# A fourth buffer for the weights of the second mixer's attention, and other copiers

## The reference, cut to what matters

```
q_r = rope_partial(q, cos, sin); k_s = rope_partial(k_s, cos, sin); k_w = rope_partial(k_w, cos, sin)
...
p = masked_softmax(jnp.einsum('bqghd,bkgd->bghqk', qb, kb) * scale, mask)
return jnp.einsum('bghqk,bkgd->bqghd', p.astype(vb.dtype), vb)
...
o = gate[..., 0:1] * heads(o_cmp) + gate[..., 1:2] * heads(o_sel) + gate[..., 2:3] * heads(o_win)
return (o.reshape(B, S, NSA_INNER) * jax.nn.silu(z)) @ w_out
```

## Time and profile before

| | |
|---|---|
| median of 3 runs | 1896.23 us |
| time of the profiled execution | 1899.72 us |
| its span | 1898.0 us |
| PE busy in the span | 1824.1 us (96%) |
| DVE, ACT, POOL busy | 1095.2, 675.3, 308.9 us |
| attention of this mixer | 626.14 to 775.6 us of the span |
| PE busy from 626 to 776 us | 125.51 us |

### The profile page before, as it was taken

The page is one execution under the profiler, slowest core; times in us unless marked ns, Lnnn a source line. Parts: engine busy times, 40 slices in busy tenths (PEclk is TensorE's granted clock), DMA queues, the critical chain, the costliest instruction groups (busy, mean ns, idle before and its releaser), DMA issues. The chain is left out here.

```text
span 1898.0 us, 36850 instructions
## 1 busy us (share of the span) xinstructions
PE 1824.1 (96%) x15870; PEld 1484.7 (78%) x15870; DVE 1095.2 (58%) x1644; ACT 675.3 (36%) x1100; POOL 308.9 (16%) x292
## 2 busy tenths in 40 slices
PE   8999999999999788999999899999999999999997
PEld 6877757688888567778888669888878888888886
DVE  4664354553257788444366887778574635354545
ACT  4334332332223577442222374433233322122342
POOL 4210011130002565320021240000001000000011
PEclk9999999999999899999999999999999999999998
DMA  5334323142223010134421100002042322322221
GB/s 191 103 111 134 136 83 133 45 190 101 90 74 111 35 37 12 49 109 138 137 102 56 48 2 4 4 3 70 4 178 92 104 104 89 111 89 89 78 100 45
DMA packets 42848, 160.87 MB, mean 85 GB/s; under 512 B 5312, under 2 KB 14528, under 8 KB 28096
## 3 DMA queue, kind: packets, MB, share of 16 engines
q1 hardware_dynamic: 28480, 143.84, 22.1%
q10 hardware_dynamic: 14208, 14.68, 2.2%
HBM read 140.42 MB, written 16.78 MB: 83 GB/s over the span
## 5 line engine op out<-in xcount | busy, mean ns | idle before, releaser
L257 DVE TENSOR_TENSOR wlo<-raw,whi 128x2048 fp32r<-128x2048 f32 (+2 forms) x113 | 251.0, 2221 | 179.2 <-ACT whi L248 178.8
L248 ACT ACTIVATE whi<-raw 128x2048 fp32r<-128x2048 f32 (+2 forms) x113 | 209.0, 1850 | 320.8 <-PE ps L283 161.4
L281 PE MATMUL ps<-act_hi,whi 128*128 128x512 f32 x616 | 243.1, 395 | 0.0
L301 PE MATMUL ps<-act_lo,whi 128*128 128x512 f32 x632 | 242.7, 393 | 0.0
L283 PE MATMUL ps<-act_hi,wlo 128*128 128x512 f32 x616 | 240.6, 391 | 0.0
L282 PE MATMUL ps<-act_lo,whi 128*128 128x512 f32 x616 | 240.5, 390 | 0.0
L300 PE MATMUL ps<-act_hi,whi 128*128 128x512 f32 x592 | 236.4, 399 | 0.0
L305 PE MATMUL ps<-act_hi,wlo 128*128 128x512 f32 x632 | 156.5, 389 | 0.0
L301 PEld LDWEIGHTS ps<-act_lo,whi 128*128 128x128 f32 x632 | 120.2, 190 | 25.9 <-issue 1.2
L305 PEld LDWEIGHTS ps<-act_hi,wlo 128*128 128x128 f32 x632 | 118.6, 188 | 24.7
L300 PEld LDWEIGHTS ps<-act_hi,whi 128*128 128x128 f32 x592 | 111.6, 188 | 32.5 <-issue 8.2
(11 more groups left out here) (550 smaller groups left out, 3474.7 us busy)
## 6 DMA issues: line engine op xcount, KB each, us to landing
raw<-stream_in SPq DMA_DIRECT2D x107, 1024.0 KB, 4.9
v_scratch<-v_out ACTq DMA_DIRECT2D x16, 256.0 KB, 3.5
z_scratch<-zt ACTq DMA_DIRECT2D x16, 256.0 KB, 2.9
mlh_v<-v_scratch SPq DMA_DIRECT2D x4, 1024.0 KB, 4.8
mlh_z<-z_scratch SPq DMA_DIRECT2D x16, 256.0 KB, 2.6
cmp_w<-cmp_w_in SPq DMA_DIRECT2D x2, 2048.0 KB, 11.3
z_scratch<-in_zt ACTq DMA_DIRECT2D x16, 256.0 KB, 3.2
mix_g<-z_scratch SPq DMA_DIRECT2D x16, 256.0 KB, 6.6
```

What stands on the lines that cost most here:

```text
L248: act.activation(k.whi[b % 2][:, 0:n], k.raw[b % RAW_SLOTS][:, 0:n], ACT.Copy).then_inc(k.hi_done, 1)
L257: dve.tensor_tensor(k.wlo[b % 2][:, 0:n], k.raw[b % RAW_SLOTS][:, 0:n], k.whi[b % 2][:, 0:n].bitcast(F32), ALU.subtract).then_inc(k.lo_don ...
L281: pe.matmul(bank, hi, x_hi, start=(x == 0), stop=False)
L301: pe.matmul(bank, hi, x_lo, start=False, stop=False)
```

## The change

- `p` gets a fourth buffer, and the distance between exponentials and turn grows by one: in turn n PE now does the turn of n-3, and the value product of n-5 and n-4 at odd n; ACT and DVE copy unit n-3. DVE's product with `z` stands at n%4 = 0.
- For 384 keys ACT copies both banks, in two instructions; DVE copies only for 256 and 128 keys (`COPIES = 2`).
- POOL scales by a product of two tensors, the second a column spread over the keys, in place of a product with a scalar.
- The fourth buffer takes the place of the high part of the queries 2 and 3, which moves into a raw weight buffer that the projection has read by then. Their split leaves ACT and DVE in the projection and becomes POOL's first work in the attention: two conversions and two subtractions.

```diff
-    k.q_hi = [k.region(f"nsa_q_hi{i}", [P, 2, S], F32R, at) for i, at in enumerate((62.5, 28))]
+    k.q_hi = [k.region("nsa_q_hi0", [P, 2, S], F32R, 62.5), k.at("nsa_q_hi1", [P, 2, S], F32R, 60 + 8 * (b1 % RAW_SLOTS))]
...
-    high_at = (17, 18, 23, 23, 24, 24, 25, 25)
+    high_at = (17, 18, 23, 23, None, 24, None, 25)
...
+    DEEP, COPIES = 4, 2
+    p = k.region("att_p", [P, DEEP, 2, S], F32, 16)
...
+            for t in (2, 3):
+                high(t)
+                low(t)
...
-                pool.tensor_scalar(p[:, m % 3, 0, 0:L], p[:, m % 3, 0, 0:L], sm(32, m)[:, 0:1], None, ALU.mult) \
-                    .then_inc(s["scaled0"], 1)
+                x = p[:, m % DEEP, 0, 0:L]
+                pool.tensor_tensor(x, x, sm(32, m)[:, 0:1].to_broadcast([P, L]), ALU.mult).then_inc(s["scaled0"], 1)
...
-                if 2 <= n < U + 2:
-                    m = n - 2
+                if DEEP - 1 <= n < U + DEEP - 1:
+                    m = n - DEEP + 1
...
-                if n >= 4 and n % 2 == 0:
-                    c = n // 2 - 2
+                if n > DEEP and n % 2:
+                    c = (n - DEEP) // 2
...
+                        if units[m][1] >= COPIES:
+                            out, src = turned(m, 0)
+                            act.activation(out, src, ACT.Copy)
                         out, src = turned(m, 1)
                         act.activation(out, src, ACT.Copy).then_inc(s["pt1"], 1)
...
-                if n >= 7 and n % 4 == 3:
-                    u = (n - 7) // 4
+                if n >= 8 and n % 4 == 0:
+                    u = (n - 8) // 4
...
-                if 2 <= n < U + 2 and units[n - 2][1] < TT - 1:
-                    m = n - 2
+                if DEEP - 1 <= n < U + DEEP - 1 and units[n - DEEP + 1][1] < COPIES:
+                    m = n - DEEP + 1
```

More of the change, by code:

```diff
@@ L1630, in score_high @@
                     act.wait_ge(s["ptr"], TT)
-                if n == 4:
-                    act.wait_ge(s["tr"], TT)
                 act.activation(hi, whole, ACT.Copy).then_inc(s["score_hi"], 1)
@@ L1687, in score_low @@
                 whole, hi, lo = parts(n)
-                dve.wait_ge(s["score_hi"], n + 1)
+                dve.wait_ge(s["score_hi"], 1 + sum(at is not None for at in high_at[:n]))
                 dve.tensor_tensor(lo, whole, hi.bitcast(F32), ALU.subtract)
@@ L1766, in _ @@
                 for n in range(8):
-                    if high_at[n] == t - 1:
+                    if high_at[n] is not None and high_at[n] == t - 1:
                         score_low(n)
@@ L1784, in stage_nsa_attention @@
     nc = k.nc
-    p = k.region("att_p", [P, 3, 2, S], F32, 16)
+    DEEP, COPIES = 4, 2
+    p = k.region("att_p", [P, DEEP, 2, S], F32, 16)
     pt = [k.at(f"att_pt{i}", [P, 2, 2, S], F32, at) for i, at in enumerate((84, 100))]
@@ L1807, in copied @@
         eng.wait_ge(s["pt1"], m + 1)
-        own = sum(i < TT - 1 for _, i, _ in units[:m + 1])
+        own = sum(i < COPIES for _, i, _ in units[:m + 1])
         if own:
@@ L1828, in low @@
             def low(t):
-                pool.wait_ge(s["q_hi"], t - 3)
+                pool.wait_ge(s["q_hi"], t - 1)
                 pool.tensor_tensor(k.q_lo[:, t, :], k.q[:, t, :], query_high(t).bitcast(F32), ALU.subtract) \
                     .then_inc(s["q_lo"], 1)
+            for t in (2, 3):
+                high(t)
+                low(t)
             for m in range(U):
@@ L1865, in scores @@
                                   start=(half == 0), stop=False, skip_group_check=True)
-                if t >= 4:
-                    pe.wait_ge(s["q_lo"], t - 3)
+                if t >= 2:
+                    pe.wait_ge(s["q_lo"], t - 1)
                 at, x = slice(i * P, (i + 1) * P), t // 4
@@ L1877, in _ @@
             scores(0)
-            for n in range(U + 3):
+            for n in range(U + DEEP):
                 if n + 1 < U:
                     scores(n + 1)
-                if 2 <= n < U + 2:
-                    m = n - 2
+                if DEEP - 1 <= n < U + DEEP - 1:
+                    m = n - DEEP + 1
                     i = units[m][1]
@@ L1891, in _ @@
                                 rows, at = rows_half(half), (TT * e + j) * P // 2
-                                last = pe.transpose(k.ps[:, 4 + half, at:at + P // 2], p[rows, m % 3, e, j * P:(j + 1) * P],
+                                last = pe.transpose(k.ps[:, 4 + half, at:at + P // 2], p[rows, m % DEEP, e, j * P:(j + 1) * P],
                                                     k.const("ident")[rows, rows])
                     last.then_inc(s["tr_mm"], 1)
-                if n >= 4 and n % 2 == 0:
-                    c = n // 2 - 2
+                if n > DEEP and n % 2:
+                    c = (n - DEEP) // 2
                     u = c // 2
@@ L1925, in high @@
                     act.activation(k.act_hi[:, 4 * gp + 2 * e + x, :], y[:, x, e, :], ACT.Copy).then_inc(s["y_hi"], 1)
-            for n in range(U + 2):
+            for n in range(U + DEEP - 1):
                 if n < U:
@@ L1933, in _ @@
                     for e in range(2):
-                        if n >= 3:
-                            act.wait_ge(s["tr_mm"], n - 2)
-                        act.activation(p[:, n % 3, e, 0:L], k.ps[:, 2 * (n % 2) + e, 0:L], ACT.Exp,
+                        if n >= DEEP:
+                            act.wait_ge(s["tr_mm"], n - DEEP + 1)
+                        act.activation(p[:, n % DEEP, e, 0:L], k.ps[:, 2 * (n % 2) + e, 0:L], ACT.Exp,
                                        bias=sm(0, n)[:, e:e + 1],
                                        accum_out=sm(8, n)[:, e:e + 1]).then_inc(s["exp_done"], 1)
-                if n >= 2:
-                    m = n - 2
+                if n >= DEEP - 1:
+                    m = n - DEEP + 1
                     L = length(m)
@@ L1968, in low @@
                     dve.tensor_tensor(k.act_lo[:, tile, :], y[:, x, e, :], k.act_hi[:, tile, :].bitcast(F32), ALU.subtract)                         .then_inc(s["y_lo"], 1)
-            for n in range(U + 4):
+            for n in range(U + DEEP + 1):
                 if n < U:
@@ L2002, in _ @@
                     L = length(m)
-                    dve.tensor_scalar(p[:, m % 3, 1, 0:L], p[:, m % 3, 1, 0:L], sm(32, m)[:, 1:2], None, ALU.mult) \
+                    dve.tensor_scalar(p[:, m % DEEP, 1, 0:L], p[:, m % DEEP, 1, 0:L], sm(32, m)[:, 1:2], None, ALU.mult) \
                         .then_inc(s["scaled1"], 1)
-                if 2 <= n < U + 2 and units[n - 2][1] < TT - 1:
-                    m = n - 2
+                if DEEP - 1 <= n < U + DEEP - 1 and units[n - DEEP + 1][1] < COPIES:
+                    m = n - DEEP + 1
                     L = length(m)
```

## The result

The changed kernel takes 1911.68 us (median of 6 runs, 1906.23 to 1914.8) against 1899.78 (6 runs, 1896.23 to 1901.25) for the kernel before on the same chip: ratio 1.0065, 95% interval 1.0047 to 1.0082. It is slower, by some 12 us where I had forecast no change. The profiled execution has a span of 1909.4 us, where before had 1898.0.

What follows compares the result with a forecast made beforehand. PE was taken as the attention's bound (125.5 of 150 us busy), with DVE and ACT setting the pace at round openings. Terms -1.7 + 1.8 - 0.6 + 0 = -0.5 us gave 1895.7 us, range 1889 to 1901.

Steps and rivals of the forecast that it cites:

- POOL's product: POOL's scaling in the attention: ends 0.2 us earlier or up to 0.7, nobody waits for it; taken as 0.
- A new lock comes with the new form: POOL's product against DVE's scaling, 16 units of 512 keys: 0 to plus 0.1 us a unit, taken as 0.
- Rival C: Slower: POOL takes the lock first, DVE's scaling held 1.18 us at 16 units, half felt; +9, 1905 us; chance 0.07.
- The sign that I gave for C: In the profile after, DVE's weight products over 0.5 us in many units would mean POOL takes the lock first.
- One more unit of distance and the copies: Attention rounds: fewer waits against smaller filler, dearer opening and ACT's copies; minus 0.1 us a round, taken as 0.
- The copies' term: ACT copying 384 keys alone: next turn 0.33 us later at two places a round, plus 0.66 us.
- the dearer opening: Opening of a round, 512-key units meeting 128-key turns: plus 0.3 us for its two pairs.
- The start: Start of the attention: first turn to first value product moves by one unit, plus 1.8 us; bounds 0.5 and 2.8.
- start and end: Attention: plus 1.8 us for the later first value product, minus 0.6 for earlier last scores at the end.
- The projection: Projection ahead of attention: removed subtractions let the last eviction come earlier, minus 1.7 us; 0.6 if rotation's transfers come late.
- A: Faster: waits for scaling at the turns were the brake; -9, 1887 us, or half, 1891.5; chance 0.25.
- B: Slower: ACT's second copy becomes the bound, up to 0.73 us at 16 places; +7, 1903 us; chance 0.13.

Runs made afterwards that it cites:

- a_late: The changed kernel with a one-element fill on POOL between its wait and its product: 1898.51 us, ratio 0.9996 to the kernel before.
- a_scalar: The changed kernel with POOL's scaling back in the scalar form: 1899.6 us, ratio 0.9994 to the kernel before.
- even_scalar: a_scalar with one head's half of a value product behind each turn, not both heads' behind every second: 1889.53 us, ratio 0.9949 to the kernel before.
- a_scalar_c3: a_scalar with COPIES = 3, so ACT and DVE share the copies of 384 keys again: 1898.54 us, ratio 0.999 to the kernel before.
- b_product: The kernel before with only POOL's scaling changed to a product with a spread column: 1915.39 us, ratio 1.0086 to the kernel before.

## Why the prediction was wrong

**The step that failed** is the last sentences of *POOL's product*: "DVE's scaling is issued first, POOL's is held until it is over", costed at 0. What I took for granted is that of two instructions released by one semaphore the one whose record starts first has the port. The rows show the reverse at 0.04 us (after), and the order that I assumed at 0.08 us (a_late). What failed is the order, and with it the cost: DVE's scaling was held at all 64 units, 1.37 us for 0.49 at 512 keys. The round came to 38.09 us, beyond the 36 that I had named as the sign of a wrong prediction.

Behind that step stands a second error. That the product form holds DVE was read rightly from the earlier trace rows. That the scalar form doesn't was read from the earlier trace rows and does not hold for the instruction that matters: those rows show DVE's small weight product, begun 1.40 us into POOL's 1.86, and the scaling right behind it, at 674.00, was held. "A new lock comes with the new form" is therefore wrong; the form changed who has the lock. The trace of before had the pair meeting in all 64 units, with POOL's record 0.06 us or more behind DVE's and DVE first each time. It could not say what happens at 0.04 us, so both outcomes had to be priced. Rival C had the mechanism and the place and a chance of 0.07, on the evidence of record starts alone. If the order was as good as open, it should have had about half, and the range should have gone past 1905. The sign that I gave for C, weight products over 0.5 us, did not show (their mean is 170 ns in after, 204 before): what was held is the scaling behind them.

C's +9 us compares with +12 measured. The rest of the 7 us between its 1905 and the 1911.68 is the base: three runs of before had 1896.23, six have 1899.78. C counted 1.18 us, half felt, at 16 places. Measured: 0.87 us more a scaling (1365 less 493) at 512 keys, and 0.67, 0.45 and 0.24 at the others. Against a_scalar the attention is 14.2 us longer. That 16 times 0.87 is 13.9 is a coincidence and no proof: with the same held scalings in each, the round behind unit 18 is 2.81 us longer than a_scalar's and the next, from unit 34 to unit 50, 5.71 (41.85 for 36.14). In that one PE's granted clock fell twice from 2.4 to 1.2 GHz (1.00 and 0.50 in the rows). These are after, around the second fall, and then a_scalar, which has the full clock there; after `us`, the first column is PE's busy time, the third DVE's:

```profile
714.35:724.59 10.24, 7.59 (x131) 6.15 (x129) 9.96 (x19) 8.14 (x20) 3.46 (x4) 1.00 0.47 156
724.59:728.00 3.41, 3.41 (x38) 3.29 (x39) 0.88 (x2) 2.54 (x10) 0.06 (x1) 0.50 0.00 0
```

```profile
642.00:773.00 131.00, 108.98 (x1886) 92.41 (x1882) 98.59 (x284) 96.24 (x313) 79.30 (x67) 1.00 0.07 22
```

From 724.59 to 728.00 PE has no pause and DVE little to do, and the pair that lies there takes 6.01 us for 4.43. So a part of the 14 us is PE's slower clock, not DVE's list; how large a part, no run separates.

**The rest of the change** can be read in a_scalar, which has all of it but the product: 1899.6 against 1901.28, ratio 0.9994 with an interval that holds 1. The forecast of these parts, -0.5 us, lies within what that interval allows. Its terms fared unevenly.

- *One more unit of distance and the copies.* PE's waits for POOL are gone, as described, but the turns stand idle nearly as long as before, 11.8 us for 12.4: 3.6 is put down to DVE's scaling (2.4 before), 3.1 to DVE's copies and 2.6 and 2.4 to ACT's, at most 0.6 and 0.7 at one turn. The round from unit 18 to 34 takes 35.28 us against 35.11; I had -0.1 and took 0. The copies' term, +0.66, compares with 35.28 less 34.55 = 0.73. Exponentials cost PE 13.2 us in a_scalar and 11.4 before, which is in line with the dearer opening that I had.
- *The start.* The first value product comes 14.47 us after the first scores in a_scalar (16.39 after; the earlier trace rows 13.07): +1.4 where I said +1.8. But it was no loss: unit 18 is reached in 40.17 us after the first scores, before it was 41.01. What the value product gives up, the scores ahead of it take. The step counted a delay of one instruction as a delay of the stage. The whole attention is 0.8 us shorter in a_scalar, where start and end made +1.2. Part of that may be the clock: from the first scores on PE had the lower one for 7.0 us in a_scalar (to 628.96, and from 635.79 to 639.20), for 8.5 us before (to 634.67) and for 3.4 more at 740.49.
- *The projection.* The instruction at 612.19, 1.77 us long, did shrink as worked out, and the eviction behind it begins at 612.07. But the rotation behind that waits for its transfer:

```profile
611.47 0.68 DVE L1687 TENSOR_TENSOR k_lo<-k_rot,k_hi 128x512 fp32r<-128x512 f32 x1
612.07 0.68 DVE L1760 TENSOR_TENSOR nsa_zt<-ps,norm_nsa_root 128x512 f32<-128x512 f32 x1
614.42 0.69 DVE L1677 TENSOR_TENSOR nsa_turned<-nsa_turned,consts 128x512 f32<-128x512 f32 x1 [1.67 <-DMA nsa_turned<-nsa_q]
...
620.48 0.68 DVE L1760 TENSOR_TENSOR nsa_zt<-ps,norm_nsa_root 128x512 f32<-128x512 f32 x1
625.09 0.28 PE L1866 MATMUL ps<-causal_bf,ident_bf 64*128 64x128 bf16 x1 [5.65 <-SPq L194]
```

The last eviction is 1.3 us earlier and PE's gap 0.9 us shorter (5.65 for 6.57; 0.6 in a_scalar, 6.02). The lower bound that I named for this very reason, 0.6, was the better value than the 1.7 that I took.

**The other rivals.** A (the waits for scaling were the brake) is half right in a way that the change could not reach: evening out PE's turns takes these waits away and brings 10 us, and one more buffer doesn't. My argument against A, that the copy ends last behind the earlier trace rows, was right as far as it went: in even_scalar both kinds of waits shrank together, once the turns stood apart. B (ACT's second copy as the bound) did not come: taking the copy away again (a_scalar_c3) gave 1.1 us where B had priced it at 11.7.

**The port.** The Trainium skill (SBUF — State Buffer, the section SBUF: two separate sides) has the port pair shared by VectorE and GpSimd as an exclusive lock, taken by whichever starts first and held for the whole instruction; on VectorE's side it names instructions with two SBUF inputs and those in a two-port mode, of which I had weighed only the first. For the two scalings the rows agree with either form of POOL's: one is held for the other (1.37 us with the product ahead, 0.54 with the end of a scaling by a scalar ahead; 1.30 instead of 1.04 for the product behind). "Starts first" can't be read from the records: at 0.04 us the later record had the lock. "For the whole instruction" doesn't fit DVE's weight product, which kept its 0.16 us inside POOL's 1.86. VectorE and GpSimd, then, meet at this port and not only at semaphores.

## What to carry to other kernels

A shorter instruction on GpSimd can be the dearer one: look at what VectorE runs in the same microsecond, and who of the two gets there first. Where two engines are released by one semaphore and may lock each other out, the start of the records doesn't tell who wins; make the cheap and urgent one win by construction, by a wait on its end or a small instruction ahead of the other, which here cost nothing that could be measured and gave back some 12 us. And where PE waits for several different releasers at one kind of place, look at the spacing of PE's own work before adding buffers: half a value product behind each turn was worth 10 to 11 us with three buffers as with four.

## What the hardware showed unexpectedly

- A product of two SBUF tensors on POOL holds up DVE's scaling of a tensor by a scalar (one tensor input): 1.37 us instead of 0.49. POOL's own scaling by a scalar does so too where it is ahead: 0.54 us, ending 0.28 us behind POOL's, as with the product.
- DVE's product of two tensors of 128x2, begun 1.40 us into POOL's scaling by a scalar of 1.86 us, took its usual 0.16 us; beside POOL's subtraction it took 1.28 us.
- With the starts of the records 0.04 us apart POOL came first, at all 64 units of after and of b_product; with 0.06 us or more (the scalar form) and with 0.08 us (the product behind a fill) DVE did, at all 64 units of before, a_scalar and a_late.
- On POOL the product with a spread column takes 1.04, 0.83, 0.61 and 0.40 us for 512, 384, 256 and 128 keys when it comes first. The scaling by a scalar from the same column takes 1.87, 1.47, 1.08 and 0.70, of which its wait for DVE's scaling is a part; the product that waits takes 1.30, 1.02, 0.74 and 0.46.
- PE's granted clock fell to 1.2 GHz for 3.41 us after 10.24 us of which PE was busy for 7.59 (after, 714.35 to 728.00).
- A one-element fill on POOL takes 0.10 us.
- An ACT copy of 128x256 takes 0.38 us, where a half (128x128) took 0.28.

Not settled: what in an instruction takes the port, and so how large a head start is safe in another kernel. For the product form the runs have 0.04 and 0.08 us and nothing between; the 0.06 us are of the scalar form alone. Nor is it shown why the product's record begins 0.04 us behind DVE's and the scalar form's 0.06.
